# Two mid-kernel RMS norms reordered by token halves beside projection tiles that are visited twice

## What is computed

```python
y = branch_out(...)              # ... @ w_out
x = x + gate_x * y               # block one, residual
x = rmsnorm(x, final_norm_g)     # mid norm 1
...
h  = _modulate(_rmsnorm(x, norm1_g[l]), mod_l[0], mod_l[1])   # mid norm 2, same tokens
hc = _modulate(_rmsnorm(ctx, norm1_g[l]), mod_c[0], mod_c[1])
z = h @ w_in[l]                  # conv, gating, q, k, v parts
att = _neighbourhood_attention(...)
y = _mix_out(att, z, ...)        # ... @ w_out
x = x + mod_l[2] * y
h2 = _modulate(_rmsnorm(x, norm2_g[l]), mod_l[3], mod_l[4])   # the norm ahead of the FFN
x = x + mod_l[5] * _conv_ffn(h2, ...)
return rmsnorm(x, final_norm_g)
```

## Time and profile before

| | us |
|---|---|
| median of 3 runs | 2883.13 |
| lowest, highest | 2882.69, 2883.93 |
| the profiled execution | 2875.19 |
| its span, first to last instruction | 2873.0 |
| mean granted TensorE clock in it | 0.950 |

### The profile page before, as it was taken

One profiled execution on the slowest core, in us unless ns is written; L12 is line 12 of the kernel. 1 busy time (PEld: TensorE's weight loads), 2 busy tenths in 40 slices (PEclk: granted clock), 3 DMA queues, 4 the chain that ended last, 5 costly groups with the idle time before them and its releaser, 6 DMA issues.

```text
span 2873.0 us, 33237 instructions
## 1 busy us (share of the span) xinstructions
PE 2570.3 (89%) x12012; PEld 2055.3 (72%) x12012; DVE 1443.2 (50%) x2097; ACT 734.5 (26%) x1151; POOL 958.6 (33%) x451
## 2 busy tenths in 40 slices
PE   2799999999989879999398799989789999999997
PEld 1688787878767757876276578867567777777775
DVE  7786036666601266531639554445344444444446
ACT  2411243434300154211412254433220101101012
POOL 1233333333257423432034111102234334334434
PEclk8799999999999889999699899989989999999999
DMA  7366453444365932231111122251011111111111
GB/s 283 130 231 233 140 154 125 151 125 151 110 238 190 353 142 102 88 117 43 74 43 39 59 87 71 72 172 39 29 37 45 52 44 44 46 48 44 45 50 66
DMA packets 129190, 309.88 MB, mean 108 GB/s; under 512 B 11329, under 2 KB 60033, under 8 KB 128577
## 3 DMA queue, kind: packets, MB, share of 16 engines
q1 hardware_dynamic: 93376, 208.81, 21.9%
q10 hardware_dynamic: 35712, 99.69, 9.5%
HBM read 233.88 MB, written 69.86 MB: 106 GB/s over the span
## 4 chain that ended last, share of the span: by engine, by line
PE 51%; DVE 6%; issue 4%; ACT 2%; DVEq 0%; DMA 0%; ACTq 0%
PE pb L459 36%; PE g L2547 5%; PE g L498 2%; PE g L2620 2%; PE pb L2547 1%; PE g L2600 1%; PE g L2528 1%; DVE zcs L1948 1%; PE g L2415 1%; DMA kept_in<-cs_d 0%; PE g L2526 0%; DVE x L2227 0%; DVE hl L2168 0%; DVE xin L1598 0%; DVE zkr L1915 0%
## 5 line engine op out<-in xcount | busy, mean ns | idle before, releaser
L825 POOL TENSOR_TENSOR w_hi<-w_raw,one 128x1024 fp32r<-128x1024 f32 x177 | 370.6, 2094 | 1823.9 <-PE pb L459 1417.4
L459 PE MATMUL pb<-xh,w_hi 128*128 128x512 f32 (+1 forms) x1224 | 485.0, 396 | 83.6 <-DVE xl L1594 67.8
L828 POOL TENSOR_TENSOR w_lo<-w_raw,w_hi 128x1024 fp32r<-128x1024 f32 x177 | 481.5, 2720 | 13.9
L459 PE MATMUL pb<-xh,w_lo 128*128 128x512 f32 (+1 forms) x1224 | 476.6, 389 | 0.0
L459 PE MATMUL pb<-xl,w_hi 128*128 128x512 f32 (+1 forms) x1224 | 476.2, 389 | 0.0
L459 PEld LDWEIGHTS pb<-xh,w_hi 128*128 128x128 f32 x1224 | 234.3, 191 | 144.7 <-issue 80.5
L459 PE MATMUL pb<-mh,w_hi 128*128 128x512 f32 x704 | 281.7, 400 | 23.0 <-DVE ml L1594 23.0
L459 PE MATMUL pb<-mh,w_lo 128*128 128x512 f32 x704 | 280.5, 398 | 0.0
L459 PE MATMUL pb<-ml,w_hi 128*128 128x512 f32 x704 | 280.5, 398 | 0.0
L459 PEld LDWEIGHTS pb<-xl,w_hi 128*128 128x128 f32 x1224 | 234.7, 192 | 51.8
L459 PEld LDWEIGHTS pb<-xh,w_lo 128*128 128x128 f32 x1224 | 235.1, 192 | 49.0 <-issue 0.7
(11 more groups left out here) (331 smaller groups left out, 4498.2 us busy)
## 6 DMA issues: line engine op xcount, KB each, us to landing
w_raw<-in_wall SPq DMA_DIRECT2D x177, 512.0 KB, 3.5
mod_raw<-in_modw SPq DMA_DIRECT2D x72, 512.0 KB, 5.5
proj_d<-stage ACTq DMA_DIRECT2D x44, 512.0 KB, 2.7
at_bias<-in_bias SPq DMA_DIRECT2D x64, 192.0 KB, 2.5
proj_d<-stage ACTq DMA_DIRECT2D x13, 640.0 KB, 3.0
svt<-vt_d ACTq DMA_DIRECT2D x12, 512.0 KB, 4.8
vc<-proj_d SPq DMA_DIRECT2D x10, 512.0 KB, 5.4
vt_d<-spare_h ACTq DMA_DIRECT2D x10, 512.0 KB, 3.7
```

The lines of the kernel that those rows point to most:

```text
L459: mm = pe.matmul(pb[bank][:, 0:n], w[:, b, wc:wc + P], x[:, k, tokens], start=(count == 0), stop=(count == total - 1))
L825: nc.gpsimd.tensor_tensor(w_hi[:, b, :], w_raw[:, b, :], one[:, 0:1].to_broadcast([P, 1024]), ALU.mult).then_inc(w_high, 1)
L828: nc.gpsimd.tensor_tensor(w_lo[:, b, :], w_raw[:, b, :], w_hi[:, b, :], ALU.subtract).then_inc(w_split, 1)
```

## The change

Seen from the data, four things are different.

1. **Halves, and tiles visited twice.** T_OUT's eight weight tiles are loaded and split twice: first all eight for tokens 0 to 511, then all eight for tokens 512 to 1023. The same holds for the four tiles of T_CV (not T_SG), for the second half of w_out_2's tiles and for the first four tiles of T_FF. That makes 20 more weight tiles (NT grows by 20), and the units of these stages have a tile each.
2. **Two norms folded into one.** Norm 2 of norm 1's result needs only the mean of (g z)^2 and the mean of z^2: with m = mean z^2 + EPS and q = mean (g z)^2 the combined factor is 1/sqrt(q + EPS m). The kernel builds it as sqrt(mean((z sqrt(g^2 + EPS))^2) + EPS^2), since EPS m = mean(EPS z^2) + EPS^2 (`both_root`, `eps2`), and scales once by `both_gain`. The unfolded x of norm 1 is not formed here: `mix` goes to `xp_d` unscaled, its root to `r1_d`, and in attention's steps 48 to 63 DVE multiplies `x2` by gain and reciprocal root ahead of each W unit's add.
3. **Sums of squares on DVE and ACT instead of PE.** ACT squares each half tile into PSUM (`g`), DVE adds them up in SBUF, and PE multiplies only the sum by the mean matrix: one matmul for each mean of a half. While the second half's units run, ACT and DVE finish and normalise the first half; while the first half's units of the next stage run, the second.
4. **The context** has a norm of its own, made behind T_CV; its low parts (`ctx_low`) stand in DVE's list after tap 4, and the pieces of taps are cut anew.

The diff, cut to what is spoken of:

```diff
-T_CV, T_SG, T_PAIR, T_W2 = 83, 87, 91, 103
-T_FF = 111
-NT = T_FF + 6 * GROUPS
+T_CV, T_SG, T_PAIR, T_W2 = 91, 99, 103, 115
+T_FF = 127
+NT = T_FF + 6 * GROUPS + 4
...
                 if s == 44:
                     sp.wait_ge(d_done, W2_FIRST)
-                    sp.wait_ge(kept_out, 48)
+                    sp.wait_ge(kept_out, 96)
+                    sp.wait_ge(at_kd, 128)
+                    sp.dma_start(r1[:, :], r1_d).then_inc(kept_back, 16)
                     sp.dma_start(kept_in[:, :, :], cs_d.rearrange("t p n -> p t n")).then_inc(kept_back, 16)
...
+                act.wait_ge(a_ml, 2 * i + 2)
+                act.dma_start(mix[:, 2 * i:2 * i + 2, :], xT[:, 2 * i:2 * i + 2, :]).then_inc(kept_back, 16)
...
+            for t in range(KT):
+                out_squares(0, t)
+            out_store(0)
+            for t in range(KT):
+                out_squares(1, t)
+                if t == 0:
+                    out_roots(0)
+                if 2 <= t < 6:
+                    for k in (2 * t - 4, 2 * t - 3):
+                        out_high(0, k)
+            out_store(1)
...
+            branch_half(0, 0)
+            out_roots(1)
+            branch_half(0, 1)
+            for v in range(2, 4):
+                for k in range(4 * v - 8, 4 * v - 4):
+                    out_high(1, k)
+                branch_half(0, v)
+            act.wait_ge(kept_out, 64)
+            act.dma_start(ctx_raw[:, :, :], ctx2T).then_inc(kept_back, 16)
...
             for t in range(4):
-                read_out(T_CV + t, zcs[:, t, :], ACT.Copy if t < 2 else ACT.Sigmoid)
...
+                read_out(T_SG + t, zcs[:, 4 + t, :], ACT.Gelu_apprx_tanh)
+                for k in (3 * t, 3 * t + 1, 3 * t + 2):
+                    if k < KT:
+                        act.wait_ge(t_ready, 3 * KT + k + 1)
+                        act.activation(xh[:, k, T:TA], ctx_raw[:, k, :], ACT.Identity,
+                                       bias=modc[:, 24 + k:25 + k]).then_inc(xh_ready, 1)
...
+            for t in range(KT):
+                out_added(1, t)
+                two = (2 * t - 4, 2 * t - 3) if 2 <= t < 6 else ()
+                for k in two:
+                    out_scaled(0, k)
+                if t:
+                    out_sums(1, t)
+                if t == 1:
+                    out_reciprocal(0)
+                for k in two:
+                    out_low(0, k)
+            out_reciprocal(1)
+            out_scaled(1, 0)
+            for k in range(1, KT):
+                out_scaled(1, k)
+                out_low(1, k - 1)
+            out_low(1, KT - 1)
...
+            def out_scaled(n, k):
+
+                if k >= 3:
+                    dve.wait_ge(xl_ready, KT * (n + 1) + k - 2)
+                nc.vector.scalar_tensor_tensor(
+                    slot(n, 3 + k % 3), mix[:, k, half_of(n)], both_gain[:, k:k + 1], slot(n, 2),
+                    ALU.mult, ALU.mult).then_inc(t_ready, 1)
...
-            taps(1, 18)
+            taps(1, 5)
+            for k in range(KT):
+                ctx_low(k)
+            taps(5, 14)
             dve.wait_ge(y_pe, 1)
...
-            for n, (first, last) in enumerate(((18, 20), (20, 21), (21, 23))):
+            for n, (first, last) in enumerate(((14, 17), (17, 18), (18, 20))):
...
-            for n, (first, last) in enumerate(((23, 26), (26, 28))):
+            for n, (first, last) in enumerate(((20, 23), (23, 25))):
...
+                    nc.vector.scalar_tensor_tensor(
+                        x2[:, m, half], x2[:, m, half], col[:, COL["final_g"] + m:COL["final_g"] + m + 1],
+                        r1[:, half], ALU.mult, ALU.mult).then_inc(x1_made, 1)
...
+                if s in (45, 46):
+                    dve.wait_ge(kept_back, 112)
+                    part = r1[:, half_of(s - 45)]
+                    nc.vector.reciprocal(part, part).then_inc(rstd_ready, 1)
...
+            for t in range(KT):
+                res_added(1, t)
+                if t >= 3:
+                    res_scaled(0, t - 3)
+                if t:
+                    res_sums(1, t)
+                if t == 2:
+                    res_reciprocal(0)
+                if t >= 3:
+                    res_low(0, t - 3)
+            for k in range(5, KT):
+                res_scaled(0, k)
+                res_low(0, k)
+            res_reciprocal(1)
...
+            for n in range(2):
+                for t in range(KT):
+                    pe_half(T_OUT + KT * n + t, n, (bh, bl))
+                    if n == 1 and t == 0:
+                        out_means(0)
+            for n in range(2):
+                for v in range(4):
+                    pe_half(T_CV + 4 * n + v, n, (xh, xl), KT * (n + 1) + 1)
+                    if n == 0 and v == 0:
+                        out_means(1)
...
-            f_up(0, ready=2 * KT + 1)
+            for v in range(8):
+                pe_half(T_FF + v, v // 4, (mh, ml), KT * (v // 4 + 4) + 1)
+                if v == 0:
+                    res_mean(1)
```

## The result

The kernel with the change takes 2802.12 us (median of 4 runs, 2800.83 to 2806.61) where the kernel before, run beside it, takes 2883.53 (2882.69 to 2884.84): a ratio of 0.972, 95% interval 0.9703 to 0.9737. The forecast was 2785 with a range of 2761 to 2814, so the gain is 81.4 us, where the forecast's sum had 97.7.

The account below looks back on a forecast made before the run. TensorE bounds the kernel, so only its waits can be gained: 142.0 us removable, less 31.8 left on the path and 12.5 in the conv section, gives 97.7. Profiled 2777.5, with 7.9 to the median 2785 us; range 2761 to 2814.

Parts of the forecast that it names:

- What goes: In both norm stages, waits, mean matmuls and trickling matmuls are removable: 93.9 + 48.1 = 142.0 us.
- (a): Mean matmuls remaining for both norms and the context, at 0.43 us per 512 columns: 2.9 us.
- (b): GpSimd's split of undisturbed half-visited tiles: 5.15 us a turn fits under 5.60, so it costs nothing.
- (c): Splits beside VectorE's two-input SBUF instructions stretch: ten tiles at 1.4 us (14.0), eight at 0.4 (3.2).
- (d): The second half's own operand chain after T_OUT comes late: 2 us of waiting in T_CV, 1 in T_FF.
- A: In half-visited tiles the splits fit into VectorE's gaps, so no collision or second-half waiting cost: 2765 us, chance 0.14.
- B: GpSimd sets the pace of all 40 half-visited tiles, 7.0 us a tile: 2829 us, chance 0.14.
- Rival D: In each norm, second-half operands come too late and TensorE trickles at low clock, 12 us each: 2806 us, chance 0.11.
- The conv section: After T_CV, context work added to full VectorE leaves a five-tap debt: cost 12.5 us, bounds 6 and 18.
- (e): T_FF's first unit, three operand pairs made in series: ends near 10.7 instead of 5.6; 7.7 us with lower clock.
- (f): DMA: xp_d's two 2 MB halves go out while weight tiles are wanted every 5.6 us: 1 us.
- Rival C: GpSimd is shut out by back-to-back VectorE work at 18 tiles, slower than before: 2955 us, chance 0.03.

Follow-up runs that it names:

- e10: Changed kernel with both mid norms' inverse root and most scaled operands kept in idle PSUM banks, same result: 2776.27 us, ratio 0.9634.
- e5: Changed kernel with r1's load given its own semaphore, so both reciprocals run in attention step 45 ahead of the kept_in wait: 2799.13 us, ratio 0.9727.
- e7: Changed kernel with 18 unused mean matmuls put into TensorE's idle time ahead of the last tap: 2796.51 us, ratio 0.9707.
- e2: Changed kernel with two operand pairs normalised beside each of four W2 tiles, none left over for T_FF: 2801.81 us, ratio 0.9726.
- e13: Changed kernel with the edits of e10, e2 and e5 together: 2769.32 us, ratio 0.9604.
- e8: Changed kernel with the context's high parts made four behind each of T_SG's first two tiles, not three behind three: 2808.64 us, ratio 0.9755.
- e11: e8 with the loop of nine taps behind ctx_low cut into three loops of three: 2808.24 us, ratio 0.9745.
- e1: Changed kernel with mid-norm instructions reading their second operand from a PSUM bank, not SBUF, giving wrong norms: 2779.57 us, ratio 0.9645.
- e14: e8 with VectorE waiting, after the first tap behind ctx_low, for the split of T_PAIR's first tile: 2798.52 us, ratio 0.9709.
- its copy: The changed kernel profiled and timed a second time, unedited, as the experiments' reference: 2805.29 us, ratio 0.9733.
- e3: Changed kernel with the context's mean matmul and root one unit of T_CV earlier: 2805.79 us, ratio 0.9734.
- e12: Changed kernel with the edits of e10, e2, e5 and e7 together: 2770.74 us, ratio 0.9611.

## Why the prediction was nearly right, point by point

- **What goes** held for the first stage and was counted 3.0 us too high for the second. No block of mean matmuls of 13 to 20 us is left, and the stage from T_OUT to T_SG is 198.2 us; the prediction's figures (1255 to 1452) make it 197. The second stage was said to end at 2189.15 with its 16 units. But the 375 matmuls of that row run on into the down tile, which begins at 2186.18. So 45.1 us were removable there and not 48.1, and 139.0 in all.

```profile
2186.18 0.39 PE L459 MATMUL pb<-hh,w_hi 128*128 128x512 f32 x1
```

- **(a) Mean matmuls** were mis-sized. I divided 13.75 us by the 32 records of the earlier trace rows, but those are 16 matmuls: a 512-wide mean matmul leaves two records, as the two of `out_means` after (below) leave four. One costs 13.75/16 = 0.86 us, so (a) is 5.6 and not 2.9. Some 2 us of the difference lie in stage one, which fell 1.8 us short.

```profile
L2702 PE MATMUL g<-spare_l,mat x4: 590/592/592, 1315.6 to 1316.8; 128*128 128x512 f32 x4
```

- **(b) The split of undisturbed tiles** held: 5.60 us from unit to unit through T_OUT's first half, with GpSimd idle 1.1 to 1.3 us a turn.
- **(c) and (d) in stage one** held in their sum. The forecast has 9.8 and 2.0, 11.8 us; e10 gives back 12.1. Inside it two errors cancel, which is luck. The price per tile in steady state is 1.50 (7.10 less 5.60), for 1.4 forecast. But one step of T_OUT took 10.13 us: the reciprocal of 3.35 us ahead of it had made VectorE late, and both pairs of that step were stretched (3.86 and 4.56 us). The estimate had left that out. From T_OUT's start to its last add e10 is 7.6 us shorter, for 5.6 forecast, and from there to the end of T_SG 4.5, for 6.2. Rivals A (2765) and B (2829) are both out: A would have 5.6 us a tile everywhere, B 7.0 in the first half too. Rival D, a second half that TensorE trickles behind, did not show in stage one (waits of 2.9 us for xh and 0.9 for xl). Yet D's 2806 us lies nearer to the result than the forecast of 2785.
- **The conv section**: forecast +12.5, bounds 6 and 18, measured +9.0. VectorE reached `hpad` at 8.2 us, not 7, but `hpad` itself took 2.35 us where before it had taken 5.99, beside a split, and the arrival at ctx_low was 27.0 us after T_CV and not 29. It was stuck for the highs, as said, though by 3.45 us and not by 6.6. TensorE's wait for the taps is 17.3 us, in the forecast 15 to 23, which by the experiments says little.
- **Attention**: forecast 0, bounds -3 and +6, measured +6.7, past the upper bound. The step that failed is "the reciprocals find about as much idle each and show 1.5 to 2". VectorE's idle time in that step, 5.85 us, was its wait for `kept_in`, and the first reciprocal stood behind the same wait, so it could not be hidden there; the second had no idle time ahead of it. e5 shows 3.4 us for the two. The rest is the clock at attention's start, which no term had: 4.6 us by step 44, 4.5 by e7. The two come to more than the 6.7, and the difference lies in these steps, which had lost only 1.9; probably because the wait for `kept_in` comes a step later, as the prediction had said.
- **The norm ahead of the FFN**: the largest miss, 13.0 us, of which 3.0 are the count above and 0.9 the two mean matmuls. The other 9.1 are waits. (e) put T_FF's first unit near 10.7 us; it took 15.9. Its terms were taken from undisturbed instructions, when all through W2's second half VectorE was already late: its reciprocal came at t = 2, each of the later steps met a split (2.01, 1.69, 2.20, 1.74, 2.19 us for instructions of 0.74), and so the add of the last unit stood 3 us behind T_FF's first matmul. In T_FF the second half's operands met the splits again (up to 2.90 us each), the fourth unit's eviction was queued behind the highs until 2042.88, and the fifth unit, the first that needs the second half's operands, waited. The mechanism of (c) was thus known, and its price was charged at 0.4 us for five tiles of W2 and at 1.4 or 0.4 for six of T_FF, as if each stood alone. e10 gives back 9.2 us, and with e2's order in e13 another 6.6. That is what rival D described, at one of its two places.
- **(f) DMA** did not show: GpSimd waits for a weight load once, at the kernel's start. TensorE's one wait for w_lo, 11.5 us in T_PAIR, was 11.7 before, and agrees with the split that the taps shut out.
- **Rival C** (GpSimd shut out by an unbroken run) did not decide this kernel, but e8 and e11 show that it exists. I had priced it for tiles beside norms; it came in long runs of taps, and in the kernel after it was luck that 3.45 us of idleness fell where T_PAIR's first split came up.
- The step from the profiled execution to the median (7.9 us added) was right only for the kernel before; after, the median is 0.8 us below its profiled execution (2802.92). Stage by stage the gain is 79.8 us and at the medians 81.4.

## What to carry to other kernels

When work is moved beside other work, price it with the rows of instructions that already run beside that work, and follow the delay to the end of the chain: here the same collision cost 1.5 us a tile in the steady part of T_OUT, and 9.2 us in all around the FFN norm, where the chain had no slack. A VectorE operand that lives in an idle PSUM bank frees GpSimd beside it, at no cost in the instruction's own time (0.74 us both ways), and gave 21.3 us in the two stages where it was used; look for that before reordering. Before taking away a wait of an engine, look at who used it: the split of T_PAIR's first tile had got through in the 3.45 us that VectorE idled.

## What the runs showed of the hardware

- **A run of two-input VectorE instructions can shut GpSimd out for its whole length.** 18 taps at 1.2 us held w_hi for 21.39 us (e8) and 21.36 (e11), the last eight or nine of them for 12.26 (after). The eight taps from 1427.37 did not: w_hi at 1438.57 came up among them and was through in 2.80. In the kernel before, one unbroken run of 34 taps from 1494.26 did both: it let w_hi in at 1508.86 (2.98 us) and 1519.96 (2.83) and held it at 1535.80 for 12.31. Cutting the loop changed nothing, a wait of VectorE did. Why the same kind of run gives turns at one time and not at another stays open. The Trainium skill (SBUF - State Buffer, "Who interferes with whom") says that whoever issues first has the shared port pair for the whole instruction; here the measurement goes further, since the 21 us are 16 instructions long.
- **The granted clock took one of two patterns at the same place of the program.** Attention's first 40 us had 0.66 to 0.68, 0.81 to 0.83, 0.83 and 1.00 in before, e1, e7, e10, e11, e13 and e14, and 0.71 to 0.73, 0.50, 0.67 and 0.56 to 0.58 in after, its copy, e2, e3, e5, e8 and e12. By step 44 the kernels measured are 4.6 to 4.9 us apart (256.4 to 256.7 us from attention's mark in before, e7, e10 and e14, 261.3 in after). Kernels that differ by 1.4 us in when they reach it, e12 and e13, differ in the pattern. In e14 a dense stretch in the last of the four stages (two of 25 us) had 0.94 and 0.93 where after has 0.98 and 1.00, and that stage is 2.9 us longer. Before a gain of that size is put down to an edit, compare the granted clock at this place.
- **A 512-wide mean matmul in float32** leaves two records and takes 0.86 us at a granted clock of 1.00 (13.75 us for 16), where one of the projections' is one record and 0.233.
